# Moving two modulation sums of layer 0 from TensorE and VectorE to GpSimd in a fused decoder kernel

## The reference

```
c_act = silu(c)                                   # (1, 1024)
for l in range(2):
    mod = c_act @ ada_w[l] + ada_b[l]             # (1, 6*1024): a vector times a 1024x6144 matrix
    sh1, sc1, gt1, sh2, sc2, gt2 = split(mod, 6)
    h = rms_norm(x, norm1_g[l]) * (1 + sc1) + sh1
    x = x + gt1 * token_mixer(h, ...)             # gt1: the attention gate, part 2
    h = rms_norm(x, norm2_g[l]) * (1 + sc2) + sh2 # sh2: the second norm's shift, part 3
    x = x + gt2 * conv_gated_mlp(h, ...)
out = rms_norm(x, final_g)
```

## Time and profile before

| | us |
|---|---|
| median of 3 runs (967.64 to 969.62) | 969.6 |
| the profiled execution, its own time | 969.08 |
| its span, first to last instruction | 967.3 |
| PE busy | 943.4 |
| VectorE busy | 788.4 |
| ScalarE busy | 517.8 |
| GpSimd busy | 18.1 |

### The profile page before, as it was taken

The page is one execution under the profiler, slowest core; times in us unless marked ns, Lnnn a source line. Parts: engine busy times, 40 slices in busy tenths (PEclk is TensorE's granted clock), DMA queues, the critical chain, the costliest instruction groups (busy, mean ns, idle before and its releaser), DMA issues.

```text
span 967.3 us, 18684 instructions
## 1 busy us (share of the span) xinstructions
PE 943.4 (98%) x7695; PEld 904.2 (93%) x7695; DVE 788.4 (82%) x1168; ACT 517.8 (54%) x725; POOL 18.1 (2%) x23
## 2 busy tenths in 40 slices
PE   5899999999999999999999999999999999999997
PEld 3798899999998999999989999999999899999997
DVE  2589999978985888889895799999898688888643
ACT  3475456557345666654255655565844456665432
POOL 5000000000000000000000000000000000000001
PEclk9999999999999999999999999999999999999999
DMA  9996555666783565957994654456678455555551
GB/s 309 336 313 189 176 189 166 201 224 211 259 296 112 191 194 194 331 174 284 392 356 132 196 146 140 142 157 206 217 262 302 132 174 181 193 192 175 175 175 44
DMA packets 142515, 204.07 MB, mean 211 GB/s; under 512 B 3928, under 2 KB 114660, under 8 KB 142436
## 3 DMA queue, kind: packets, MB, share of 16 engines
q1 hardware_dynamic: 142100, 202.78, 62.6%
q10 hardware_dynamic: 336, 0.14, 0.1%
HBM read 199.76 MB, written 1.05 MB: 208 GB/s over the span
## 4 chain that ended last, share of the span: by engine, by line
PE 79%; DVE 15%; DMA 2%; ACT 2%; issue 1%; SPq 0%; DVEq 0%
PE PB L1619 17%; PE PB L1621 16%; PE PB L1620 16%; DVE wL L1039 5%; DVE buf L1145 3%; PE PB L1642 2%; PE PB L1643 2%; PE PB L1644 2%; PE SC L1621 2%; PE SC L1619 2%; PE SC L1620 2%; PE ST L1598 2%; DMA raw<-in_w_in 1%; DMA ada_pre<-in_ada_w 1%; PE TR L1621 1%
## 5 line engine op out<-in xcount | busy, mean ns | idle before, releaser
L1619 PE MATMUL PB<-hH,wH 128*128 128x256 f32 x1360 | 388.9, 286 | 0.7 <-DVE wL L1039 0.7
L1621 PE MATMUL PB<-hH,wL 128*128 128x256 f32 x1360 | 384.8, 283 | 0.0
L1620 PE MATMUL PB<-hL,wH 128*128 128x256 f32 x1360 | 384.7, 283 | 0.0
L1039 DVE TENSOR_TENSOR wL<-raw,wH 128x2048 fp32r<-128x2048 f32 (+3 forms) x152 | 322.9, 2127 | 63.8 <-ACT wH L742 59.5
L742 ACT ACTIVATE wH<-raw 128x2048 fp32r<-128x2048 f32 (+3 forms) x152 | 268.4, 1782 | 106.5 <-DMA raw<-in_w_down 53.1
L1619 PEld LDWEIGHTS PB<-hH,wH 128*128 128x128 f32 x1360 | 260.7, 192 | 3.1 <-issue 1.7
L1620 PEld LDWEIGHTS PB<-hL,wH 128*128 128x128 f32 x1360 | 260.8, 192 | 0.1
L1621 PEld LDWEIGHTS PB<-hH,wL 128*128 128x128 f32 x1360 | 260.7, 192 | 0.0
L1145 DVE SCALAR_TENSOR_TENSOR buf<-G,vec,buf 128x256 f32<-128x256 f32 x240 | 98.2, 480 | 0.3
L1399 DVE SCALAR_TENSOR_TENSOR ups<-PB,vec,ups 128x254 f32<-128x254 f32 (+1 forms) x176 | 72.6, 475 | 18.0 <-ACT ups L910 18.0
L918 ACT ACTIVATE gH<-ups 128x512 f32 (+1 forms) x22 | 13.9, 632 | 86.7 <-DVE ups L1406 86.7
(11 more groups left out here) (302 smaller groups left out, 1698.4 us busy)
## 6 DMA issues: line engine op xcount, KB each, us to landing
raw<-in_w_in SPq DMA_DIRECT2D x48, 1024.0 KB, 5.6
raw<-in_w_up SPq DMA_DIRECT2D x44, 1024.0 KB, 5.1
ada<-in_ada_w SPq DMA_DIRECT2D x35, 1024.0 KB, 8.5
raw<-in_w_down SPq DMA_DIRECT2D x22, 1024.0 KB, 4.9
ada_pre<-in_ada_w SPq DMA_DIRECT2D x8, 1024.0 KB, 13.5
raw<-in_w_o SPq DMA_DIRECT2D x8, 1024.0 KB, 6.3
raw<-in_w_out_diff SPq DMA_DIRECT2D x4, 1024.0 KB, 4.9
raw<-in_w_out_conv SPq DMA_DIRECT2D x4, 1024.0 KB, 5.0
```

Of the source, the lines that this page charges most:

```text
L1039: dve.tensor_tensor(wL[s][:, 0:size], raw[s][:, 0:size], wH[s][:, 0:size].bitcast(F32), ALU.subtract).then_inc(w_lo[s], 1)
L1619: pe.matmul(out, a, xh(k), start=first and k == 0, stop=False, skip_group_check=True)
L1620: pe.matmul(out, a, xl(k), start=False, stop=False, skip_group_check=True)
L1621: ins = pe.matmul(out, b, xh(k), start=False, stop=last and k == kt - 1, skip_group_check=True)
```

## The change

GpSimd gets both sums of layer 0. For each block it scales the two row groups by their columns of `c_col`, adds them, and adds the running sum. VectorE's `early_steps` go. PE's four `ada_step` calls of part 3 go, with ScalarE's eviction and `reduce_ada` at step 29; `reduce_shift` at step 25 reduces the finished sum instead, which lies in `ada_u`. The loads of part 3 move to steps 13, 15, 17 and 20; all but the first wait for GpSimd's step before. The late sum's first two buffers swap places, and ScalarE waits for the fifth late step ahead of writing `uH`, in both layers. VectorE's order around steps 3 to 6 changes: lambda sums and vector copies, then the rotation of the shared key (`Rkr`) in step 3, the reciprocal of the latent norms in step 4, the rotation of `Rk0` first in step 5, the row maxima of `D0` ahead of the low half in step 6, the weights of step MLA + 4 ahead of the low half too.

```diff
-ROTATE_AT = {4: ["Rq0"], 5: ["Rk0"], 7: ["Rkr"], 9: ["Rq1"], ...
+ROTATE_AT = {4: ["Rq0"], 9: ["Rq1"], ...
-ADA_STEPS = [None] * 4 + [14, 18, 22, 25] + [None] * 8
-ADA_LOADS = [None] * 4 + [n + 1 for n in ADA_STEPS[4:ADA_ONCE]] + [None] * 4 + [39, 40, 42, 41]
+ADA_LOADS = [None] * 4 + [13, 15, 17, 20] + [None] * 4 + [39, 40, 42, 41]
-ADA_REDUCE_AT = {12: 0, 29: 1, 39: 2, UP + 4 * UP_LOOPS + 1: 3}
+ADA_REDUCE_AT = {12: 0, 25: 1, 39: 2, UP + 4 * UP_LOOPS + 1: 3}
-        late_ws = [ada_u, ada[0], ada[1], ada[2]]
+        late_ws = [ada[0], ada_u, ada[1], ada[2]]
@@ load_ada, on SP
                 elif a < ADA_ONCE:
-                    sp.wait_ge(ada_used, a - ADA_PART)
+                    sp.wait_ge(shift_added, a - ADA_PART)
@@ load_late, on SP
                 if i == 0 and l == 0:
-                    sp.wait_ge(mi_full, 1)
+                    sp.wait_ge(shift_added, ADA_PART)
                 if i == 1 and l == 0:
-                    sp.wait_ge(ada_used, ADA_PART)
+                    sp.wait_ge(mi_full, 2)
@@ gpsimd, behind the mask's cast
+            pool.wait_ge(s_silu, 1)
+            for i in range(4):
+                w = early_ws[i]
+                pool.wait_ge(early_in[i], 16)
+                pool.tensor_scalar(w[:, 0, :], w[:, 0, :], c_col[:, 2 * i, 0:1], None, ALU.mult)
+                link(pool.tensor_scalar(w[:, 1, :], w[:, 1, :], c_col[:, 2 * i + 1, 0:1], None, ALU.mult))
+                ins = pool.tensor_tensor(w[:, 0, :], w[:, 0, :], w[:, 1, :], ALU.add)
+                if i:
+                    link(ins)
+                    ins = pool.tensor_tensor(w[:, 0, :], w[:, 0, :], early_ws[i - 1][:, 0, :], ALU.add)
+                ins.then_inc(early_added, 1)
+                pool.wait_ge(early_added, i + 1)
+
+            w, total = ada[0], ada_u[:, 0, :]
+            for i in range(ADA_PART):
+                pool.wait_ge(ada_in[0], 16 * (i + 1))
+                pool.tensor_scalar(w[:, 0, :], w[:, 0, :], c_col[:, 2 * i, 0:1], None, ALU.mult)
+                link(pool.tensor_scalar(w[:, 1, :], w[:, 1, :], c_col[:, 2 * i + 1, 0:1], None, ALU.mult))
+                if i == 0:
+                    pool.wait_ge(mi_full, 1)
+                    ins = pool.tensor_tensor(total, w[:, 0, :], w[:, 1, :], ALU.add)
+                else:
+                    link(pool.tensor_tensor(w[:, 0, :], w[:, 0, :], w[:, 1, :], ALU.add))
+                    ins = pool.tensor_tensor(total, total, w[:, 0, :], ALU.add)
+                ins.then_inc(shift_added, 1)
+                pool.wait_ge(shift_added, i + 1)
@@ ScalarE, step 33
                     act.wait_ge(ln_u, l + 1)
+                    act.wait_ge(late_added, 8 * l + 5)
@@ VectorE, mixer_step
                 if n == 3:
                     latent_squares(l)
-                if l == 0:
-                    early_steps(n)
-                if n == MLA + 1:
+                    if l == 0:
+                        lam_sums()
+                        flush_vectors(l)
+                        dve.wait_ge(s_table, 1)
+                    rope(l, "Rkr")
+                if n == 4:
+                    dve.wait_ge(st_read, FREE + l * len(ST_USES) + 2)
+                    link(dve.reciprocal(rdev[:, :], rdev[:, :]))
+                if n == 5:
+                    rope(l, "Rk0")
+                if n in (MLA + 1, MLA + 4):
                     weights(l, SCORES_AT[n - 1])
+                if l == 0 and n == 6:
+                    row_max(l, SCORES_AT[n])
@@ PE
-                after(early_added, 8)
+                after(early_added, 4)
+            def reduce_shift():
+
+                after(mi_read, 1)
+                after(shift_added, ADA_PART)
+                for m in range(DT):
+                    ins = pe.matmul(MI[:, 2 * m:2 * m + 2], ada_u[:, 0, m * P:(m + 1) * P], ones[:, 0:2], start=True,
                                     stop=True, skip_group_check=True)
+                ins.then_inc(mi_full, 1)
-                a = ADA_STEPS.index(n) if n in ADA_STEPS else None
-                if a is not None:
-                    if l < LAYERS - 1:
-                        ada_step(l, a)
```

More of the change, by code:

```diff
@@ L94 @@
 VALUES_INSIDE = 9
-ROTATE_AT = {4: ["Rq0"], 5: ["Rk0"], 7: ["Rkr"], 9: ["Rq1"], 10: ["Rk1"], 15: ["RM0"], 20: ["RM1"], 25: ["RM2"],
+ROTATE_AT = {4: ["Rq0"], 9: ["Rq1"], 10: ["Rk1"], 15: ["RM0"], 20: ["RM1"], 25: ["RM2"],
              30: ["RM3"]}
@@ L108 @@
 ADA_ONCE, ADA_GAP, ADA_CHUNKS = 8, 12, 16
-ADA_STEPS = [None] * 4 + [14, 18, 22, 25] + [None] * 8
-ADA_LOADS = [None] * 4 + [n + 1 for n in ADA_STEPS[4:ADA_ONCE]] + [None] * 4 + [39, 40, 42, 41]
+ADA_LOADS = [None] * 4 + [13, 15, 17, 20] + [None] * 4 + [39, 40, 42, 41]
 ADA_BUF = [0] * ADA_GAP + [1, 2, 3, 0] * 2
-ADA_EVICT_AT = {12: 0, 29: 1, UP + 4 * UP_LOOPS: 3}
-ADA_REDUCE_AT = {12: 0, 29: 1, 39: 2, UP + 4 * UP_LOOPS + 1: 3}
-assert len(ADA_STEPS) == ADA_CHUNKS and UP + 4 * UP_LOOPS == 59
+ADA_EVICT_AT = {12: 0, UP + 4 * UP_LOOPS: 3}
+ADA_REDUCE_AT = {12: 0, 25: 1, 39: 2, UP + 4 * UP_LOOPS + 1: 3}
+assert len(ADA_LOADS) == ADA_CHUNKS and UP + 4 * UP_LOOPS == 59
 EARLY_Q = 0
-EARLY_LOADS, EARLY_STEPS = [3, 4, 4, 5], [2, 2, 3, 3, 3, 3, 4, 4]
+EARLY_LOADS = [3, 4, 4, 5]
 LATE_Q = 2
@@ L153, in ada_evicts @@
 def ada_evicts(l, q):
-    return {0: 3, 1: 1, 3: l * 2 + 2}[q]
+    return {0: 2, 3: l * 2 + 1}[q]
 def ada_done(l, q):
-    return {0: 12, 1: 4, 3: l * 8 + 8}[q]
+    return {0: 8, 3: l * 8 + 4}[q]
 V_N1, V_N2, V_ADAB, V_QG, V_KVG, V_CB, V_LNG, V_LNB, V_SUB, V_FB = 0, 8, 16, 64, 67, 69, 73, 77, 81, 82
@@ L413, in trunk_kernel @@
         early_in, early_added = [sem(f"early_in{i}") for i in range(4)], sem("early_added")
+        shift_added = sem("shift_added")
         late_in, late_added = [sem(f"late_in{i}") for i in range(4)], sem("late_added")
@@ L555, in load_sum @@
                 if b < ADA_PART:
-                    sp.wait_ge(ada_used, ADA_PART + b + 1)
+                    sp.wait_ge(ada_used, b + 1)
                 else:
@@ L1190, in mixer_step @@
                 ada_work(l, n)
-                if n - 1 in SCORES_AT and n != MLA + 1:
+                if n - 1 in SCORES_AT and n not in (MLA + 1, MLA + 4):
                     weights(l, SCORES_AT[n - 1])
@@ L1216, in mixer_step @@
                     rope(l, use)
-                if n in SCORES_AT:
+                if n in SCORES_AT and (l, n) != (0, 6):
                     row_max(l, SCORES_AT[n])
                 if n == 5 - l:
-                    dve.wait_ge(st_read, FREE + l * len(ST_USES) + 2)
-                    link(dve.reciprocal(rdev[:, :], rdev[:, :]))
                     for k in range(QT + KVT):
@@ L1302, in mixer_step @@
                         merged_low(l, n)
[L1304 to L1317, removed]
             def late_steps(l, n):
@@ L1344, in ada_work @@
                         if l < LAYERS - 1:
-                            ada_end(ADA_PARTS[q], ada_order(l, q), vec)
+                            ada_end(ADA_PARTS[q], ada_order(l, q), vec, 2)
                     elif at + 1 == n:
@@ L1569, in reduce_early @@
             def reduce_early():
-                after(early_added, 8)
+                after(early_added, 4)
                 for m in range(DT):
                     ins = pe.matmul(MI[:, 2 * m:2 * m + 2], early_ws[3][:, 0, m * P:(m + 1) * P], ones[:, 0:2], start=True,
+                                    stop=True, skip_group_check=True)
+                ins.then_inc(mi_full, 1)
[4 more added lines that the diff above has]
+                    ins = pe.matmul(MI[:, 2 * m:2 * m + 2], ada_u[:, 0, m * P:(m + 1) * P], ones[:, 0:2], start=True,
                                     stop=True, skip_group_check=True)
@@ L1789, in ada_at @@
                     if l < LAYERS - 1:
-                        reduce_ada(ada_evicts(l, q))
+                        reduce_shift()
                 elif q == LATE_Q:
```

## The result

| | before | after |
|---|---|---|
| median of 5 runs each on one chip (lowest to highest) | 968.8 (967.64 to 969.62) | 998.85 (997.3 to 1000.4) |
| ratio, 95% interval | | 1.0307 [1.0295, 1.0319] |
| span of the profiled execution | 967.3 | 998.6 |
| mean granted clock | 0.994 | 0.979 |

What follows compares the result with a forecast made beforehand. VectorE was taken as narrowly the limit to 160 us, then PE. GpSimd's 73.8 us, less 9.7, 4, 6 and 6, left 48; PE's recoveries made it 43, added to 969.1: 1012 us, range 967 to 1034.

Steps and rivals of the forecast that it cites:

- The block: Layer 0's mixer: a GpSimd instruction stops VectorE instructions using SBUF for its whole remaining length; 1012 us, chance 0.72.
- means well above: Sign in the profile after: taps of 0.48 us and low halves of 2.29 us lengthen, only where GpSimd is busy.
- Rivals 1 and 2: No block for two SBUF inputs: SP's queue stalls, 967 us, chance 0.12; or GpSimd is free, 962 us, chance 0.07.
- Rival 3: VectorE and GpSimd share instead of blocking, so overlapped instructions only stretch: 982 us, chance 0.09.
- the same full block: Upper bound taken for two-input VectorE instructions: all 73.8 us of GpSimd's 16 multiplications and 14 additions stand in VectorE's way.
- start-up and one-input work: Deductions from the 73.8 us: 6 for start-up of 30 GpSimd instructions, 6 for VectorE work that can run beside GpSimd.
- VectorE slightly ahead as the limit: From 60 to 160 us VectorE, busy 98.18 of 100 us, sets the time narrowly ahead of PE's 96.19.
- at most 7.2 us: PE's largest gain if nothing replaced the removed steps: 3.8 us of lost time plus 3.4 net of its own steps.
- SP's queue: Shift loads waiting for GpSimd delay weight loads behind them; 5 us reach PE, mostly hidden under the block.
- Just in time: The second modulation load leaves SP's queue at 122.5 us, where the next weight load went out at 122.57 before.
- The clock: Stalls of PE can lower its granted clock, 0.91 in an earlier window: 1.8 us in 20, outside the sum.
- Costed at nothing: VectorE's reorder, ScalarE's new wait ahead of `uH` (2.6 us of cover) and the first late load's wait add no time.

Runs made afterwards that it cites:

- gate_add: Kernel before with the gate's sum on GpSimd, its eight multiplications left out, only seven additions kept: 972.97 us, 1.004.
- gate_none: Kernel before with the gate's sum left out: blocks loaded, neither scaled nor added, VectorE without its eight early steps: 968.76 us, 0.9995.
- shift_none: Kernel before with the shift's loads and reduction moved as in the change, GpSimd's multiplications and additions left out: 973.35 us, 1.0049.
- shift_only: Kernel before with only the shift's sum on GpSimd, its loads and reduction at the change's steps; gate stays on VectorE: 991.69 us, 1.0221.
- own_queue: Only the shift's sum on GpSimd, against the kernel before, with GpSimd instead of SP issuing the shift's four loads: 985.1 us, 1.0166.
- spread_loads: Changed kernel with the shift's four loads further apart (steps 13, 17, 21, 24), its reduction and first two late loads later: 995.17 us, 1.0263.
- the reorder: Kernel before with VectorE's new order of rotations, reciprocal, row maxima and weights alone, both sums left in place: 969.22 us, 1.0.

## Why the prediction was right or wrong

- **The block.** Right for additions: a VectorE instruction that meets one, with two inputs or a copy or scaling with one, starts its own work as the addition ends. Row maxima keep their length. The sign "means well above" held for low halves (2668 ns against 2.29 us) and hardly for taps: 521 ns against 0.48 us over 99 of them is some 4 us in all, less than two additions. Rivals 1 and 2, no block for two inputs, are out by gate_add. Rival 3, sharing, is out too: nothing stretches in proportion, though its 982 us was not farther off than my point, at 17 against 13 us.
- **The step that failed is the size of the hold**, in "the same full block" for all 73.8 us. A multiplication holds VectorE for some 0.8 us of its 2.84, not for 2.6. With 16 x 0.8 + 14 x 2.4 the holds are 46 us by estimate instead of 73.8, and my own deductions for start-up and one-input work (6 and 6) make 34 of them; VectorE stood 33.8. So near a match is partly luck: the rows above give 0.14 us of start-up an addition, 2 us in all. The prices of the instructions themselves were nearly right: 2.84 against 2.6 and 2.4 against 2.3.
- **The slack.** I deducted 9.7 us of removed steps and 4 in which VectorE stands anyway, 13.7; gate_none shows 13.4, so this part of the sum was right. Wrong was the reading "VectorE slightly ahead as the limit": PE gained nothing when the 9.7 us went. And PE didn't win back the 3.4 us of its removed steps, the other half of "at most 7.2 us": shift_none, without them, is 4.2 us slower.
- **SP's queue.** I had 5 us reach PE, hidden under the block. They are not all hidden: 6.3 us in shift_only by own_queue, and about 4 in the kernel after by spread_loads. "Just in time" failed first: the second modulation load left at 124.19 even in shift_none, and in the kernel after at 140.07, since it waits for the early reduction, itself 13 us late. So the too large holds were in part made good by a queue costed at nothing.
- **The clock.** I put it at 1.8 us, in the range and not in the sum. It is a third of the loss: 10.3 us of the 33 up to 252 us are PE being busy longer. So the forecast's 45 us of PE's waits for `wL` and `W`, where they are 23.3, was twice too large, and the total came nearer only because this term was missing.
- **GpSimd's +75 us** became +97: it also waits for VectorE, as the multiplication of 4.76 us shows; the longest took 7.38. The first sum stretched to 47 us (48.44 to 95.43), where I had 50.
- **Costed at nothing**, and rightly: the reorder (969.22 us). The wait ahead of `uH` shows nothing either: `uH` is written 24.4 us behind the matmul of 251.85, at 276.23, and was written 25.3 us behind it before, at 244.34.

The parts, measured apart, are the gate's 12.0 us, the shift's 16.1 without the queue, and the queue's 6.3: 34, against 30 together. Why the two together cost 4 less was not tried.

## What to carry to other kernels

GpSimd is not a free engine while VectorE runs instructions with two SBUF inputs: price a GpSimd instruction by how long it holds VectorE, and set that against VectorE's slack in that very stretch, which leaving the work out measures in one run. Busy shares of two engines over 100 us don't tell which is the limit. When a load is moved onto a buffer that another engine must free, look at what stands behind it in the queue, and at what its reader has queued behind its own wait.

## What the hardware showed

- Additions 128x1024 on GpSimd (2.4 us) held VectorE's two-input instructions to their end; multiplications by a column of the same size (2.84 us) for 0.8 us; fills (1.81 us) not at all, yet fills held copies and scalings with one input by 1.2 to 1.6 us.
- The hold goes both ways: a multiplication of 2.84 us alone was recorded with up to 7.38 us beside VectorE's taps and low halves.
- The multiplication is dearer than the addition of the same size, 2.84 against 2.4 us, though it reads half as much.
- PE's granted clock averaged 0.83 in the 60 us in which PE was idle for 15.5, and 0.97 in the next 60, in which it was full. From 44 to 252 us (219 before), 22.7 us more of waits came with 10.3 us more of busy time.
